# A two-layer decoder trunk with retrieved experts: both fp16 pieces of a gate table through one load of the one-hot matrix

## What is computed

```python
def peer_ffn(x, w_q, sub_keys, u, v):
    q = (x @ w_q).reshape(b, s, PEER_HEADS, 2, PEER_DQ // 2)
    sc = jnp.einsum('bshcd,hcnd->bshcn', q, sub_keys)
    ...
    top_s, pos = lax.top_k(cand, PEER_TOPK)          # 16 experts per token and head
    eidx = jnp.take_along_axis(cidx, pos, axis=-1)   # i1 * 128 + i2
    gate = jax.nn.softmax(top_s, axis=-1)
    ...
        hid = jax.nn.gelu(jnp.einsum('btd,bthkd->bthk', xb, u[eb]), approximate=False)
        w = gb * hid
        return jnp.einsum('bthk,bthkd->btd', w, v[eb])
```

## Time and profile before

| what | value |
|---|---|
| median of three executions | 2198.21 us |
| the profiled execution, its own time | 2195.7 us |
| span in its trace | 2193.8 us |
| TensorE's matmuls busy | 2109.5 us, 96% |
| VectorE, ScalarE, GpSimd busy | 70%, 43%, 39% |
| granted TensorE clock, mean | 0.984 of 2.4 GHz |
| read from HBM | 340 MB, mean 155 GB/s over the span |
| spreads that build the tables of the last two quarters | 64 (16 batches x 2 tables x 2 layers) |

### The profile page before, as it was taken

The page is one execution under the profiler, slowest core; times in us unless marked ns, Lnnn a source line. Parts: engine busy times, 40 slices in busy tenths (PEclk is TensorE's granted clock), DMA queues, the critical chain, the costliest instruction groups (busy, mean ns, idle before and its releaser), DMA issues.

```text
span 2193.8 us, 46574 instructions
## 1 busy us (share of the span) xinstructions
PE 2109.5 (96%) x18012; PEld 1922.2 (88%) x18034; DVE 1540.7 (70%) x2683; ACT 952.5 (43%) x1399; POOL 856.7 (39%) x360
## 2 busy tenths in 40 slices
PE   6989988999999999999989999899999999999998
PEld 6978988888989898999888789898898989899997
DVE  5572698998876887566354618989887777776663
ACT  5563434334444444433555534343434343433444
POOL 4624640004343434444555257300034343434444
PEclk9999999999999999999999899999999999999999
DMA  6403443444444444455443034434444444445553
GB/s 236 154 20 136 157 152 112 158 153 172 172 172 173 172 172 172 176 187 191 159 166 137 4 134 157 150 117 155 156 171 174 171 174 171 172 172 190 185 181 113
DMA packets 48523, 342.62 MB, mean 156 GB/s; under 512 B 5536, under 2 KB 6560, under 8 KB 7200
## 3 DMA queue, kind: packets, MB, share of 16 engines
q1 hardware_dynamic: 47984, 337.93, 43.0%
q10 hardware_dynamic: 432, 3.21, 0.4%
HBM read 340.08 MB, written 1.05 MB: 155 GB/s over the span
## 4 chain that ended last, share of the span: by engine, by line
PE 87%; DVE 5%; ACT 3%; issue 2%; POOL 2%; DMA 1%; SPq 0%; DVEq 0%; ACTq 0%; POOLq 0%
PE psum L448 26%; PE psum L449 25%; PE psum L450 25%; PE psum L766 4%; POOL wl L372 1%; ACT wh L360 1%; DMA ring<-stream 1%; PE psum L462 1%; PE psum L667 1%; DVE wl L372 1%; PE psum L591 1%; PE psum L738 1%; ACT arena L887 1%; PE psum L659 1%; DVE arena L1630 1%
## 5 line engine op out<-in xcount | busy, mean ns | idle before, releaser
L372 POOL TENSOR_TENSOR wl<-ring,wh 128x1024 fp32r<-128x1024 f32 x336 | 831.9, 2496 | 1277.0 <-ACT wh L360 1277.0
L360 ACT ACTIVATE wh<-ring 128x1024 fp32r<-128x1024 f32 x628 | 627.7, 1046 | 396.4 <-PE psum L450 384.0
L448 PE MATMUL psum<-xh,wh 128*128 128x256 f32 (+1 forms) x2320 | 668.6, 288 | 13.2 <-DVE wl L372 12.2
L449 PE MATMUL psum<-xl,wh 128*128 128x256 f32 (+1 forms) x2320 | 659.5, 284 | 0.0
L450 PE MATMUL psum<-xh,wl 128*128 128x256 f32 (+1 forms) x2320 | 659.4, 284 | 0.0
L448 PEld LDWEIGHTS psum<-xh,wh 128*128 128x128 f32 (+1 forms) x2320 | 446.6, 192 | 18.5 <-issue 14.0
L449 PEld LDWEIGHTS psum<-xl,wh 128*128 128x128 f32 (+1 forms) x2320 | 446.9, 193 | 1.3
L450 PEld LDWEIGHTS psum<-xh,wl 128*128 128x128 f32 (+1 forms) x2320 | 446.7, 193 | 0.2
L372 DVE TENSOR_TENSOR wl<-ring,wh 128x1024 fp32r<-128x1024 f32 x292 | 362.2, 1280 | 100.8 <-ACT wh L360 100.8
L448 PE MATMUL psum<-wh,Wh 128*128 128x512 f32 (+1 forms) x1056 | 412.5, 391 | 3.7 <-POOL Wl L1204 2.0
L449 PE MATMUL psum<-wl,Wh 128*128 128x512 f32 (+1 forms) x1056 | 408.7, 387 | 0.0
(11 more groups left out here) (229 smaller groups left out, 2119.1 us busy)
## 6 DMA issues: line engine op xcount, KB each, us to landing
ring<-stream SPq DMA_DIRECT2D x318, 1024.0 KB, 4.8
arena<-keys ACTq DMA_DIRECT2D x2, 1024.0 KB, 6.7
smr<-rows SPq DMA_DIRECT2D x1, 1090.0 KB, 11.0
smr<-rows ACTq DMA_DIRECT2D x1, 1090.0 KB, 5.2
h<-x SPq DMA_DIRECT2D x1, 1024.0 KB, 5.0
out<-h SPq DMA_DIRECT2D x4, 256.0 KB, 2.1
sm<-cols SPq DMA_DIRECT2D x1, 728.0 KB, 9.0
kst<-consts SPq DMA_DIRECT2D x1, 495.0 KB, 7.7
```

The lines of the kernel that those rows point to most:

```text
L360: nc.scalar.activation(wh[:, buffer_of(L, n), c], ring[:, (L * SLOTS + n) % RING, c], ACT.Copy).then_inc(hi_ok, 1)
L372: eng.tensor_tensor(wl[:, b, c], ring[:, (L * SLOTS + n) % RING, c], wh[:, b, c].bitcast(F32), ALU.subtract).then_inc(done, 1)
L448: pe.matmul(o, a[0], b[0], start=start, stop=False, **kw)
L449: pe.matmul(o, a[0], b[1], start=False, stop=False, **kw)
```

## The change

For the tables of quarters 2 and 3 alone (those of quarters 0 and 1 are built as before):

- TensorE's new `spread_wide` issues one matmul a token in place of two: the same stationary `Bh`, and 64 moving columns, the 32 of each piece. Nothing accumulates. The result of a batch is twice as wide and fills banks 6 and 7 together (8 tokens in each, 64 columns a token). The wait for `g_ok` is gone from TensorE's side.
- ScalarE's `gates_out` reads every token's first 32 columns out of the two banks, scales and writes them to the table as before.
- VectorE's new `pieces_added` waits for that eviction, reads the other 32 columns of each token from PSUM, scales them and adds the table's values in SBUF (one scalar_tensor_tensor of 512 elements), and raises `gm_ok`.
- VectorE's order in a pair of quarters 1 and 2 becomes `low(p)`, `onehots` of the next batch, `weigh(p+1)`, `pieces_added`. Against the order before, this is the same sequence with `pieces_added` between `weigh(p+1)` and `low(p+1)`. At the end of a quarter it waits for `gm_ok` before the first `weigh` of the next. In quarter 3 the sequence is the one of before, its loop cut at another place.
- That banks 6 and 7 are free for the next spread is ensured by order: it stands behind `weighted(p+1)`, which waits for `low(p+1)`, which VectorE does behind `pieces_added`.

```diff
--- before.py
+++ after.py
@@ -333,6 +333,7 @@
         q_ok, sc_ps, sc_ok = sem("q_ok"), sem("sc_ps"), sem("sc_ok")
         ge_in, ge_ok, prod_ok, rout_ok, rout_ps, rout_dve = (sem(n) for n in ("ge_in", "ge_ok", "prod_ok", "rout_ok", "rout_ps", "rout_dve"))
         b_ok, e_ok, a_ok, g_ps, g_ok = (sem(n) for n in ("b_ok", "e_ok", "a_ok", "g_ps", "g_ok"))
+        gm_ok = sem("gm_ok")
         gelu_ok, w_ok, acc_ps = sem("gelu_ok"), sem("w_ok"), sem("acc_ps")
         sg_ok, ph_ok, pl_ok = sem("sg_ok"), sem("ph_ok"), sem("pl_ok")
         dve_step, act_step = sem("dve_step"), sem("act_step")
@@ -398,6 +399,10 @@
         def chunk_bank(i):
 
             return 4 + i % 4
+
+        def both_pieces():
+
+            return psum[:, 6:8, :].rearrange("p b n -> p (b n)").rearrange("p (t k e) -> p k e t", k=PIECES, e=QI)
 
         block = ctx.enter_context(nc.Block())
 
@@ -767,6 +772,15 @@
                                             start=(k == 0), stop=(k == PIECES - 1))
                     ins.then_inc(g_ps, 1)
 
+                def spread_wide(n, par):
+
+                    pe.wait_ge(b_ok, n + 1)
+                    pe.wait_ge(a_ok, n + 1)
+                    for i in range(TB):
+                        ins = pe.matmul(bank(6 + 2 * i // TB, PIECES, QI, at=i % (TB // 2) * PIECES * QI), Bh[:, par, i, :],
+                                        Ah[:, par, :, i, :], start=True, stop=True)
+                    ins.then_inc(g_ps, 1)
+
                 def hidden(i, p, step=2):
 
                     w = [a.rearrange("p (e k n) -> p e k n", e=2, k=DC) for a in parts(L, u_slot(p))]
@@ -833,7 +847,7 @@
                             hidden(i, p + 1)
                             weighted(i, p)
                             if quarter < QUARTERS - 1:
-                                spread(q0 + (quarter + 1) * NB + 2 * i + k, k)
+                                spread_wide(q0 + (quarter + 1) * NB + 2 * i + k, k)
                 hidden(0, PAIRS - 1)
                 weighted(0, PAIRS - 2)
                 weighted(0, PAIRS - 1)
@@ -1095,7 +1109,7 @@
                     act.wait_ge(g_ps, (L * QUARTERS + quarter) * NB + step * i + n + 1)
                     buf = ar((quarter % 2) * SEQ * QI, QI, SEQ)
                     act.activation(buf[:, :, bass.ds((step * i + n) * TB, TB)],
-                                   bank(6 + n % 2, TB, QI).rearrange("p t e -> p e t"),
+                                   (bank(6 + n % 2, TB, QI).rearrange("p t e -> p e t") if quarter < 2 else both_pieces()[:, 0]),
                                    ACT.Copy, scale=1.0 / G_SCALE).then_inc(g_ok, 1)
 
                 def lead(i, ks):
@@ -1678,6 +1692,13 @@
                 low(0, 0)
                 dve.wait_ge(g_ok, (L * QUARTERS + 1) * NB)
 
+                def pieces_added(quarter, i, n):
+
+                    dve.wait_ge(g_ok, (L * QUARTERS + quarter) * NB + 2 * i + n + 1)
+                    buf = ar((quarter % 2) * SEQ * QI, QI, SEQ)[:, :, bass.ds((2 * i + n) * TB, TB)]
+                    dve.scalar_tensor_tensor(out=buf, in0=both_pieces()[:, 1], scalar=1.0 / G_SCALE, in1=buf,
+                                             op0=ALU.mult, op1=ALU.add).then_inc(gm_ok, 1)
+
                 def first_quarter(i):
                     for k in range(4):
                         weigh(i, k, 4)
@@ -1691,23 +1712,32 @@
                 with dve.Fori(1, QP // 4 - 1) as i:
                     first_quarter(i)
                 first_quarter(QP // 4 - 1)
-                for quarter in range(1, QUARTERS):
-                    dve.wait_ge(g_ok, (L * QUARTERS + quarter + 1) * NB)
-
-                    def body(i):
-                        for k in range(2):
-                            weigh(i, quarter * QP + k)
+                dve.wait_ge(g_ok, (L * QUARTERS + 2) * NB)
+                weigh(0, QP)
+                for quarter in range(1, QUARTERS - 1):
+
+                    def body(i, ks):
+                        for k in ks:
                             low(i, quarter * QP + k)
-                            if quarter < QUARTERS - 1:
-                                ahead(quarter, i, k)
+                            ahead(quarter, i, k)
+                            weigh(i, quarter * QP + k + 1)
+                            pieces_added(quarter + 1, i, k)
 
                     with dve.Fori(0, QP // 2 - 1) as i:
-                        body(i)
-                    if quarter < QUARTERS - 1:
-                        body(QP // 2 - 1)
-                for p in (PAIRS - 2, PAIRS - 1):
-                    weigh(0, p)
-                    low(0, p)
+                        body(i, range(2))
+                    body(QP // 2 - 1, range(1))
+                    low(0, (quarter + 1) * QP - 1)
+                    ahead(quarter, QP // 2 - 1, 1)
+                    pieces_added(quarter + 1, QP // 2 - 1, 1)
+                    dve.wait_ge(gm_ok, (2 * L + quarter) * NB)
+                    weigh(0, (quarter + 1) * QP)
+                with dve.Fori(0, QP // 2 - 1) as i:
+                    for k in range(2):
+                        low(i, (QUARTERS - 1) * QP + k)
+                        weigh(i, (QUARTERS - 1) * QP + k + 1)
+                low(0, PAIRS - 2)
+                weigh(0, PAIRS - 1)
+                low(0, PAIRS - 1)
                 dve.wait_ge(acc_ps, L + 1)
                 for half in range(2):
                     for t in range(T):
```

## The result

| | kernel before | changed kernel |
|---|---|---|
| median of four executions | 2196.87 us (2190.53 to 2203.95) | 2176.04 us (2172.81 to 2178.28) |
| ratio, with its 95% interval | | 0.9911 (0.9888 to 0.9934) |
| the profiled execution: own time, span | 2195.7, 2193.8 us | 2177.9, 2176.1 us |

The account below looks back on a forecast made before the run. The prediction took TensorE's matmul stream, busy throughout the pairs of quarter 2, as the bound. Its terms, -21.8 - 2.4 + 2.4 = -21.8 us, gave a median of 2176.4 us, range 2167.5 to 2189.5 us.

Parts of the forecast that it names:

- The spread: TensorE's 64 spreads in quarters 1 and 2: 16 matmuls at 29.2 ns, 0.34 us less each, -21.8 us.
- Rival (a): Spread matmuls: weight load and columns add up, 38.6 ns each, -9.9 us in all, 2188.3 us; chance 0.14.
- rival (c): Spread matmuls: loads not hidden behind columns read in strips, spacing doubles to 50.6 ns, no gain, 2200.6 us; chance 0.04.
- rival (b): Spread matmuls: an issue or load floor of 25.3 ns still holds at 64 columns, -25.8 us, 2172.4 us; chance 0.17.
- The loop's end: TensorE's branch after every second spread: 0.15 us uncovered, nothing to 4.8 us back, half taken, -2.4 us.
- The addition in the pair: VectorE's pieces_added before low(p+1): 0.77 us each, 64 times, covered, so nothing on the path.
- The 0.8 us of reserve: How early the first half of low is ready for TensorE's weighted when the one-hots are caught by GpSimd.
- The change of quarter: Four changes of quarter: addition and gm_ok wait come before weigh and low, TensorE stalls 0.6 us each, +2.4 us.

## Why the prediction was right, point by point

- **The spread, -21.8 us.** Right in size and reason. 29.2 ns was taken and 29.2 ns measured; 0.338 us a spread, 64 times, is 21.6 us. Rival (a), load plus columns, and rival (c) fell with that row. The floor of rival (b) exists, and the kernel with the first piece alone shows it at 32 columns, but it doesn't reach 64. Of the Trainium skill's two statements (TensorE: Matmul & The Clock Gate, section Back-to-back issue gap) the trace follows the formula, about 29 ns, and not the table's 60 cycles.
- **The loop's end, -2.4 us.** That the 0.15 us are the loop's end is shown by the kernel with half as many ends. That slower instructions still queued cover it now is argued only. The size was taken at half. All of it came back: 31 pairs are 12.6 us shorter, of which the spreads are 10.5 us, and 15 loop ends at 0.16 us, 2.4 us, less one stall of 0.31 us, are the rest. In both layers and at all 32 ends that is about 4.8 us.
- **The addition in the pair, 0.** Right: 0.69 us, 64 times, without a wait of TensorE in a full pair. The 0.8 us of reserve was about 0.5. The prediction's reason why a delay can't add up from pair to pair, that GpSimd does two instructions a pair, isn't enough: with 0.6 us more, one late change of quarter made the 15 pairs behind it about 0.12 us longer each. Its support, that the addition never takes longer, held (maximum 0.693 us), but no addition ran beside GpSimd, in the kernels that add twice and three times neither, so what the Trainium skill says of one SBUF input (SBUF — State Buffer, section Who interferes with whom) is not tested here.
- **The change of quarter, +2.4 us.** Right in place and cause, twice too large: 0.31 us each, 1.2 us in all. The addition was 0.08 us shorter than taken, and started 0.03 us behind the eviction, where 0.41 us had been carried over from the earlier trace rows. That leaves 0.2 us of wait, as measured, and the longer first matmul is the rest.
- **What the prediction did not have.** "If quarter 3 or anything outside quarters 1 and 2 changes its length, my account is wrong." One thing did: the second layer's projection and attention, +4.9 us on average, at the places where the granted clock is lower. By that sign the account wasn't complete. The sum is -21.6 - 4.8 + 1.2 + 4.9 = -20.3 us; measured by the medians, -20.8. The forecast of -21.8 came near it because three errors nearly cancel: 2.4 us too little at the loop ends, 1.2 us too much at the changes of quarter, and the 4.9 us that it didn't have. That the time itself, 2176.0 us, is within 0.4 us of the forecast is luck once more, since the median of the kernel before came out 1.3 us lower with a fourth execution.

## What to carry to other kernels

Where TensorE is the bound and issues many short matmuls, count them and not only their columns. By an estimate from the three spacings here (25.3 ns, and columns plus 2.5 ns, meet near 55 columns) a 16-bit matmul with its own weight load costs a floor below that, and one saved can be worth it even when another engine has to add the results. Before giving that engine the work, measure its reserve by doing the added work twice or three times; here 0.7 us was free in a pair, 1.3 us was free only until something came late once, and 1.9 us made the kernel slower than it had been, because it pushed other instructions into another engine's stretch. A gain of one per cent shown pair by pair can lose a fifth of itself in an untouched stage, so cut the whole span into stages and take several traces before calling that noise.

## What the runs showed of the hardware that was not expected

- A loop's end on TensorE costs 0.15 us behind 64 short instructions (32 loads, 32 matmuls, 0.82 us) and nothing behind 32 (0.48 or 0.41 us), though these are over sooner. Why is argued and not shown.
- The product in `weigh` took 0.69 us in all 128 cases before (L1648 there). Shifted by the addition, it meets GpSimd too, in two cases of the changed kernel (L1662, ns min/median/max):

```profile
L1662 DVE TENSOR_TENSOR arena<-arena x128: 678/683/2884, 396.6 to 2125.5; 128x512 f32<-128x512 f32 x112, 128x512 f32 x16
```

- The second layer's projection and attention take 532.7 to 542.3 us with the places at which the clock falls to 1.2 GHz. The time was the same within 0.6 us in four traces of the changed kernel and within 0.1 us in three of four of the kernel before, and it differs between kernels with the same instructions there.
